# Two-block forward pass on one core: the second mixer's convolution offset, decay masks and time-step chain, rewritten and reordered

## What is computed

```python
CHUNK, SSM_HEADS, SSM_HEAD_DIM, D_STATE, CONV_WIDTH = 128, 16, 64, 128, 4
def causal_depthwise_conv(u, w, b):
    y = lax.conv_general_dilated(u, w[:, None, :], window_strides=(1,), padding=[(CONV_WIDTH - 1, 0)], ...)
    return y + b
def segsum_exp(a):
    cs = jnp.cumsum(a, axis=-1)
    diff = cs[..., :, None] - cs[..., None, :]
    return jnp.exp(jnp.where(mask, diff, -jnp.inf))          # mask: lower triangle
def ssd_chunked(xs, dt, a_neg, bm, cm):
    xg = (xs.astype(jnp.float32) * dt[..., None]).reshape(...)
    a = jnp.transpose((dt * a_neg).reshape(...), ...)
    a_cs = jnp.cumsum(a, axis=-1)
    cb = jnp.einsum('bclgn,bcsgn->bcgls', cc, bc)
    m_mat = cb[:, :, :, None] * segsum_exp(a)
    y_diag = jnp.einsum('bcgels,bcsgep->bclgep', m_mat, xg)
    ...                                                      # and the state that chunk 0 hands to chunk 1
def hybrid_mixer(...):
    xbc = jax.nn.silu(causal_depthwise_conv(xbc, conv_w, conv_b))
    dt = jax.nn.softplus(dt.astype(jnp.float32) + dt_bias.astype(jnp.float32))
    y = ssd_chunked(xs, dt, a_neg, bm, cm) + d_skip[:, None] * xs
    y = y.reshape(...) * jax.nn.silu(z)
    y = rmsnorm(y.reshape(bsz, s, SSM_GROUPS, gsize), ssm_norm.reshape(SSM_GROUPS, gsize))
    return jnp.concatenate([attn, y], axis=-1) @ w_out
```

## Time and profile before

| | us |
|---|---|
| time, median of 3 runs (lowest, highest) | 1499.72 (1497.44, 1502.09) |
| the profiled execution's own time | 1500.76 |
| its span, first to last instruction | 1499.0 |
| TensorE busy | 1470.0 (98%) |
| VectorE, ScalarE, GpSimd busy | 953.1 (64%), 785.0 (52%), 90.8 (6%) |
| mean granted TensorE clock, share of full | 0.995 |

### The profile page before, as it was taken

The page is one execution under the profiler, slowest core; times in us unless marked ns, Lnnn a source line. Parts: engine busy times, 40 slices in busy tenths (PEclk is TensorE's granted clock), DMA queues, the critical chain, the costliest instruction groups (busy, mean ns, idle before and its releaser), DMA issues.

```text
span 1499.0 us, 19461 instructions
## 1 busy us (share of the span) xinstructions
PE 1470.0 (98%) x7541; PEld 1255.5 (84%) x7541; DVE 953.1 (64%) x1356; ACT 785.0 (52%) x1232; POOL 90.8 (6%) x94
## 2 busy tenths in 40 slices
PE   8999999999999999999999989999999999999998
PEld 8888888888888888888888978888888988888886
DVE  5698765565568867555555797655555697755553
ACT  6764454444467644544445665444445574554443
POOL 0122100000002220000000010000000010000000
PEclk9999999999999999999999999999999999999999
DMA  8643356655465435566664343566654343456551
GB/s 283 214 143 125 121 162 195 201 192 184 129 210 159 141 99 179 176 207 185 192 179 119 116 140 99 169 203 207 188 184 137 107 140 118 150 188 184 188 190 57
DMA packets 178700, 245.86 MB, mean 164 GB/s; under 512 B 18976, under 2 KB 130096, under 8 KB 178608
## 3 DMA queue, kind: packets, MB, share of 16 engines
q1 hardware_dynamic: 178416, 244.54, 52.7%
q10 hardware_dynamic: 192, 0.08, 0.0%
HBM read 243.52 MB, written 1.05 MB: 163 GB/s over the span
## 4 chain that ended last, share of the span: by engine, by line
PE 80%; DVE 13%; ACT 4%; issue 2%; DVEq 0%; ACTq 0%
PE acc L546 14%; PE acc L540 14%; PE acc L543 14%; PE misc L540 10%; PE misc L543 10%; PE misc L546 10%; DVE w_lo L1321 5%; DVE arena L1696 2%; PE misc L637 1%; PE misc L734 1%; ACT arena L1019 1%; PE misc L863 1%; ACT w_hi L952 1%; PE misc L805 1%; PE misc L686 1%
## 5 line engine op out<-in xcount | busy, mean ns | idle before, releaser
L1321 DVE TENSOR_TENSOR w_lo<-w_raw,w_hi 128x1024 fp32r<-128x1024 f32 (+3 forms) x472 | 563.3, 1205 | 319.4 <-ACT w_hi L952 317.8
L952 ACT ACTIVATE w_hi<-w_raw 128x1024 fp32r<-128x1024 f32 (+3 forms) x472 | 480.8, 1029 | 287.5 <-PE misc L546 164.1
L540 PE MATMUL acc<-w_hi,h_hi 128*128 128x512 f32 (+3 forms) x832 | 210.4, 376 | 1.0 <-ACT h_hi L991 1.0
L546 PE MATMUL acc<-w_hi,h_lo 128*128 128x512 f32 (+3 forms) x832 | 201.4, 365 | 1.4 <-DVE arena L1672 1.4
L543 PE MATMUL acc<-w_lo,h_hi 128*128 128x512 f32 (+3 forms) x832 | 201.5, 365 | 0.0
L540 PE MATMUL misc<-w_hi,h_hi 128*128 128x512 f32 x640 | 175.5, 396 | 0.0
L543 PE MATMUL misc<-w_lo,h_hi 128*128 128x512 f32 x640 | 171.5, 390 | 0.0
L546 PE MATMUL misc<-w_hi,h_lo 128*128 128x512 f32 x640 | 171.5, 390 | 0.0
L546 PEld LDWEIGHTS acc<-w_hi,h_lo 128*128 128x128 f32 x832 | 148.5, 189 | 23.3 <-DVE arena L1672 1.7
L543 PEld LDWEIGHTS acc<-w_lo,h_hi 128*128 128x128 f32 x832 | 148.9, 189 | 22.0
L540 PEld LDWEIGHTS acc<-w_hi,h_hi 128*128 128x128 f32 x832 | 144.3, 191 | 23.2 <-issue 1.8
(11 more groups left out here) (200 smaller groups left out, 1298.6 us busy)
## 6 DMA issues: line engine op xcount, KB each, us to landing
w_raw<-in_w_in SPq DMA_DIRECT2D x92, 512.0 KB, 3.8
w_raw<-in_w_gate SPq DMA_DIRECT2D x176, 256.0 KB, 2.9
w_raw<-in_w_up SPq DMA_DIRECT2D x176, 256.0 KB, 3.1
w_raw<-in_w_down SPq DMA_DIRECT2D x88, 512.0 KB, 3.6
w_raw<-in_w_out SPq DMA_DIRECT2D x40, 512.0 KB, 3.6
w_raw<-in_w_in SPq DMA_DIRECT2D x32, 388.0 KB, 3.3
w_raw<-in_w_in SPq DMA_DIRECT2D x16, 336.0 KB, 4.2
w_raw<-in_w_proj_a SPq DMA_DIRECT2D x8, 512.0 KB, 4.0
```

The costliest lines, as they stand in the source:

```text
L540: pe.matmul(dst, st[0][:, k, t * P:(t + 1) * P], rhs, start=first, stop=False)
L546: return pe.matmul(dst, st[1][:, k, t * P:(t + 1) * P], rhs, start=False, stop=last)
L952: act.activation(w_hi[:, g % RING, 0:w], w_raw[:, g % RING, 0:w], ACT.Copy)\
L1321: dve.tensor_tensor(w_lo[:, g % RING, 0:w], w_raw[:, g % RING, 0:w], w_hi[:, g % RING, 0:w].bitcast(F32), ALU.subtract)\
```

## The change

The tap 3 and offset of the convolution go to ScalarE: `channels` gets two Identity instructions with scale and bias that read the PSUM bank directly, and `convolve` loses its first two. The time step `dt` no longer multiplies the states: its logarithm is taken (a second Ln on ScalarE) and added, as a bias, inside the exponentials, so that `xdt`, the four VectorE multiplications behind it and GpSimd's four are gone, and TensorE's `y` steps read `xs`. The exponentials of the diagonal blocks become four of 128 columns with a bias of their own, in place of two of 2x128 columns. One `min` of 2x2x128 columns replaces the four subtract-and-min. The skip term becomes one multiply-add for each head in `head_pair_out`, two in place of one. The small `dt` steps move ahead of `convolve(3)` on VectorE and ahead of `channels(4)` on ScalarE; `cs` moves in TensorE's order from behind `cb1` to between two slots of `z0`, `cr0` to ahead of the first slot of `z1`. A one-element Exp is placed behind the `z0` product. The start and stop flags of the slot matmuls are derived from the slot's place; they come out the same.

```diff
@@ plan_b, TensorE's order
-        xd3 attT0 attT1 xd3 xT3 xd3 xd3 z0 xT4 xT5 z0 z0 xsT0 xsT1 xsT2 xsT3 z0 z1 cb0 cb1 cs cr0 cr1
+        xd3 attT0 attT1 xd3 xT3 xd3 xd3 z0 xT4 xT5 z0 cs z0 xsT0 xsT1 xsT2 xsT3 z0 cr0 z1 cb0 cb1 cr1
@@ TensorE, y
                     pe.wait_ge(*DV_.at(layer, f"M{i}"))
+                    if i in (0, 4):
+                        pe.wait_ge(*AC.at(layer, f"xs{2 + i // 4}"))
-                        pe.matmul(b[:, u * SP:(u + 1) * SP], E[:, 0:P], xdt[:, 0, cols], start=True, stop=True)
+                        pe.matmul(b[:, u * SP:(u + 1) * SP], E[:, 0:P], xs[:, 0, cols], start=True, stop=True)
@@ ScalarE, channels(i)
+                    for k in (2 * i, 2 * i + 1):
+                        act.activation(cv[:, k, :], b[:, (k % 2) * T:(k % 2 + 1) * T], ACT.Identity,
+                                       scale=conv[:, 36 + k:37 + k], bias=conv[:, 48 + k:49 + k])\
+                            .then_inc(*AC.mark(f"xT{i}"))
@@ ScalarE, decays(hp), in place of two Exp over 2x128
+                        for part, bias in ((0, dt_v[:, hd:hd + 1]), (2, dt_v[:, 16 + hd:17 + hd])):
+                            v = E[:, u, part * P:(part + 1) * P]
+                            act.activation(v, v, ACT.Exp, bias=bias).then_inc(*AC.mark(f"ex{hp}"))
@@ ScalarE, order
-                channels(4)
-                channels(5)
                 act.wait_ge(*DV_.at(layer, "dt_u"))
                 act.activation(dt_v, dt_v, ACT.Exp).then_inc(*AC.mark())
                 act.activation(ea, prm[:, 16:32], ACT.Exp).then_inc(*AC.mark())
                 act.wait_ge(*AC.now(layer))
                 act.activation(dt_v, dt_v, ACT.Ln, bias=1.0).then_inc(*AC.mark("dt_ln"))
+                channels(4)
+                act.wait_ge(*DV_.at(layer, "dt"))
+                act.activation(dt_v, dt_m, ACT.Ln).then_inc(*AC.mark("log_dt"))
+                channels(5)
...
+                act.activation(early[:, :], halves[:, 0:1], ACT.Exp).then_inc(*AC.mark())
@@ VectorE, exponents(hp), in place of four tensor_scalar
+                    diagonal = Ex[j % 3].rearrange("p u (b t) -> p u b t", b=3)[:, :, 0:3:2, :]
+                    own = cs[:, 0:32].rearrange("p (t h a) -> p h t a", t=NT, a=1)[:, 2 * hp:2 * hp + 2, :, :]
+                    dve.tensor_tensor(diagonal, b[:, :].rearrange("p (u t q) -> p u t q", u=2, t=NT),
+                                      bc(own, [P, 2, NT, P]), ALU.min).then_inc(*DV_.mark(f"cr{hp}"))
@@ VectorE, order
+                convolve(4)
+                b = wait_bank(layer, "cs")
+                dve.tensor_copy(cs, b[:, 0:48]).then_inc(*DV_.mark("cs"))
+                dve.wait_ge(*AC.at(layer, "log_dt"))
+                dve.wait_ge(*DV_.now(layer))
+                dve.tensor_tensor(dt_v, dt_v, cs[:, 0:32], ALU.subtract).then_inc(*DV_.mark())
...
                 convolve(5)
-                    dve.tensor_tensor(xdt[:, t, 512 * half:512 * half + 512].rearrange("p (h d) -> p h d", h=8),
-                                      b[:, :].rearrange("p (h d) -> p h d", h=8), bc(r, [P, 8, SP]), ALU.mult)\
@@ VectorE, head_pair_out(hp)
+                        dve.scalar_tensor_tensor(out=ys[:, :, cols], in0=xs[:, :, cols],
+                                                 scalar=prm[:, 32 + hd:33 + hd], in1=src, op0=ALU.mult, op1=ALU.add)\
@@ GpSimd, body_b
-                    pool.tensor_tensor(v, v, bc(dsk, [P, 8, SP]), ALU.mult).then_inc(*PO.mark("xsd"))
```

More of the change, by code:

```diff
@@ L241 @@
 READ_B.update({f"wo{i}": ("dve", f"wo{i}.t1") for i in range(2)})
-ACT_READS = ("hqT", "hfT", "qkT", "PT", "GX", "xT", "cr")
+ACT_READS = ("hqT", "hfT", "qkT", "PT", "GX", "xT", "xsT", "cr")
+PAIRS = tuple(range(8))
 def reader(block, name):
@@ L583, in run_slot @@
                         at = kk * c.ncols
-                        cells.append((acc[2 * o.pair[name] + t][:, 0:c.ncols], st, tile, t, k,
+                        cells.append((acc[2 * o.pair[name] + t][:, 0:c.ncols], st, tile, t, i == 0 and kk == 0,
+                                      i == len(c.slots) - 1 and kk == nk - 1,
                                       w_hi[:, g % RING, at:at + c.ncols], w_lo[:, g % RING, at:at + c.ncols]))
@@ L601, in sweep @@
                         pe.wait_ge(*DV_.at(layer, f"nT{n}"))
-                    for dst, st, tile, t, k, hi, lo in cells:
-                        mm = low(dst, st, tile, t, hi, k == c.ktiles - 1)
+                    for dst, st, tile, t, first, last, hi, lo in cells:
+                        mm = low(dst, st, tile, t, hi, last)
                     return mm
@@ L1234, in body_b @@
                 for i in range(4):
[L1235 to L1238, removed]
+                    turned_states(i)
                 conv_silu(2)
                 copy_product(layer, "z0", lambda t: zs[:, t, 0:512], ACT.Silu, "x")
[L1242 to L1266, removed]
+                act.activation(early[:, :], halves[:, 0:1], ACT.Exp).then_inc(*AC.mark())
@@ L1267, in body_b @@
+                for hp in range(4):
+                    decays(hp)
+                copy_product(layer, "z1", lambda t: zs[:, t, 512:1024], rms="x")
+                decays(4)
+                decays(5)
+                split_until(layer, ORD[1].before["misc", "cr6"] + LOOK)
+                group_squares(0)
+                decays(6)
+                decays(7)
                 operand(layer, "ssT0")
                 operand(layer, "ssT1")
-                split_until(layer, ORD[1].before["misc", f"y{SH // 2 - 1}"] + LOOK)
+                split_until(layer, ORD[1].before["misc", "y7"] + LOOK)
@@ L1729, in body_b @@
                 dve.tensor_tensor(dt_v, dt_u, dt_a, ALU.min).then_inc(*DV_.mark("dt_u"))
-                convolve(4)
+                convolve(3)
                 dve.wait_ge(*AC.at(layer, "dt_ln"))
-                dve.tensor_tensor(dt_m, dt_m, dt_v, ALU.add).then_inc(*DV_.mark("dt"))
+                dve.scalar_tensor_tensor(out=dt_m, in0=dt_u, scalar=1e-37, in1=dt_v, op0=ALU.max, op1=ALU.add)\
+                    .then_inc(*DV_.mark("dt"))
                 dve.wait_ge(*DV_.now(layer))
```

116 lines of the change are left out of this document (62 added, 54 removed).

## The result

The changed kernel takes 1489.47 us (median of 4 runs, 1488.46 to 1489.76); runs of the kernel before, made beside it, take 1498.58 (1497.31 to 1502.09). The ratio is 0.9934, with a 95% interval of 0.9921 to 0.9947. The prediction said 1489.7 and a range of 1485.5 to 1495.5.

What follows compares the result with a forecast made beforehand. TensorE, busy 98% of the span, was taken as the bound, so only its gaps and half-clock stretches could yield: 4.4 + 6.1 = 10.5 us off 1500.76, less half of 1.04, gives 1489.7 us, range 1485.5 to 1495.5.

Steps and rivals of the forecast that it cites:

- The stretch: TensorE from `xsT0` to `y1`, second mixer: 20.25 us in layer 1 instead of 26.33; gains 4.4 and 6.1, together 10.5.
- The first Silu: ScalarE ahead of `xsT0`: Silu starts 8.7 us after the last `xd3` copies, as now, at 877.3 to 877.7.
- The wait ahead of xsT3: New TensorE wait of 1.45 us per layer for VectorE's copy of `cs`, ends 0 and 2.0; rival without it, chance 0.06.
- cb0, cr1, y0: TensorE's waits ahead of `cb0` and `cr1` go; `y0` has slack 1.3 us; rival, `y0` waits 1.7 per layer, chance 0.10.
- The clock: Rival: TensorE's clock still falls to half behind the `xsT3` wait, 1.6 us a layer, 1491.3 or 1492.9; chance 0.18.
- The attention part: Identities of `channels(0)` to `(2)` near `O4`: cost 0, range -0.3 to 1.6 us; rival 1492.9 to 1495, chance 0.07.
- The step on `xsT0`: TensorE ahead of `xsT0`: Identities use up the early `dt`'s gain; `cs` (0.59 us) fills the idle 0.76 there.
- the one on GpSimd: GpSimd's multiplications go at no price, nothing waits for them; VectorE beside them gets 1.7 us back.
- The 1.7: VectorE time regained: two lo took 4.05 us beside GpSimd's multiplications, 2.35 elsewhere.
- The sum: Total over both layers: 10.5 us off the profiled 1500.76 gives 1490.3, then half of 1.04 off: 1489.7 us.
- The table loads: ScalarE: next activation 1.30 us after a load starts, no 1.38 draining; rival, extra loads make it slower, chance 0.04.

Runs made afterwards that it cites:

- the kernel without waits: Changed kernel with tap 3 and offset back on VectorE and the copy of `cs` no longer behind one slot's lo: 1484.85 us.
- the first experiment: Changed kernel with one slot's lo no longer ahead of VectorE's copy of `cs`: 1485.76 us.
- The experiments on the one minimum and the early Exp: Changed kernel with four 128-column minimum steps in place of one of 512: 1489.9 us; changed kernel without the one-element Exp: 1490.14 us.

## Why the prediction was right, and where it was not

**The stretch: right.** 20.25 us were forecast, 20.18 and 20.19 measured; 10.5 us of gain forecast, 10.65 measured. Two small errors cancel in it: the work itself is 18.10 us by the kernel without waits, not 18.95 - 0.59 = 18.36, and the 0.2 that TensorE takes to run again was left out for the wait ahead of `xsT3`. The time, 1489.7 against 1489.47, agrees more closely than the runs can tell, and that is luck: the forecast was 10.0 below a median of 1499.72, the measured gain is 9.1 from a median of 1498.58, and taking off half of the 1.04 between the profiled execution and the median was a choice.

**The first Silu: right.** 8.7 us behind the last `xd3` copies were forecast; it is 876.72 - 867.91 = 8.81 in ScalarE's timeline:

```profile
867.91 1.06 ACT L1070 ACTIVATE arena<-acc,small 128x388 f32<-128x388 f32 x2 [0.86 <-PE acc L547]
...
872.88 1.01 ACT L1200 ACTIVATE arena<-misc,conv 128x256 f32<-128x256 f32 x2
...
875.43 1.28 ACT L1206 ACT_TABLE_LOAD   x1
876.72 2.00 ACT L1206 ACTIVATE arena<-arena 128x1024 f32<-128x1024 f32 x2
```

An Identity takes 565 ns on average and steps by about 0.45, where 0.40 was taken and 0.37 to 0.48 were the ends. The Trainium skill (ScalarE: Activation LUTs, What ACT_TABLE_LOAD costs) prices each operand that is a pointer at about 93 ns; with two of them and 256 columns an estimate by its figures is 585 ns, which this trace bears out.

**The wait ahead of xsT3: right.** 1.45 forecast, 1.33 and 1.32 measured, and by the first experiment the copy of `cs` is its cause. The price of its place is more than the wait: 3.7 us in the medians, 3.0 of them in the two stretches; the rest is no more than the runs' spread.

**cb0, cr1, y0: right.** M ends at 892.0 and TensorE is at `y0` at 893.04, a slack of 1.0 where 1.3 was said. The forecast had no lo ahead of M, which holds only by the edit to the exponents of pair 1 shown above. The chain on ScalarE held: the decays began at 888.80 (889.3 forecast), and the four new Exp step by 0.29 where 0.25 was taken. The experiments on the one minimum and the early Exp use up 0.4 and 0.2 of the slack without harm.

**The clock: the rival did not come.** A wait of 1.33 left the granted clock at 1.00; so did 1.37 ahead of `cr0` with 0.99 ahead of `y0`, and 1.6 ahead of `y0` alone. It fell behind waits of 4.87 and 3.71. In between, equal waits came out differently in the two layers of one run. Two of 1.5 in the kernel before were followed by 0.50 in layer 0; in layer 1 they left the clock at 1.00, and it fell behind a third, of 1.66, that ended at 1247.22:

```profile
1240.00:1247.00 7.00, 4.10 (x22) 3.08 (x21) 5.36 (x18) 3.34 (x9) 0.00 (x0) 1.00 0.45 150
1248.00:1249.00 1.00, 1.00 (x7) 1.00 (x6) 0.72 (x1) 0.24 (x1) 0.00 (x0) 0.50 0.00 0
```

With GpSimd's work cut and the order moved, 1.88 ahead of `cr0` left it at 1.00 in layer 0, and 1.87 was followed by 0.50 in layer 1. With `cr0` left behind `cb1`, 2.24 ahead of `cb0` left it at 1.00 in layer 0, and 2.26 was followed by 0.50 in layer 1. So the length of a wait does not say by itself whether the clock falls. That it would hold was the likelier case, not a thing the rows of before could show.

**The attention part: right, though its row looks worse.** `O4` is listed with a wait of 0.71 in place of 0.18:

```profile
853.51 1.10 PE L664 MATMUL misc<-arena 128*128 128x64 f32 x8 [0.71 <-ACT arena L1029]
```

But `O0` to `O5` takes 857.02 - 832.29 = 24.73 us in place of 24.59. The wait has taken over from one of 0.15 ahead of `O3`, which is gone, and the price is 0.14 in this layer against a forecast of 0; layer 1's attention part lies in the stretch of 324.40 before and 324.32 after. A longer wait in the list is no loss until the steps around it start later.

**Where the reasoning failed: the share of the parts.** The step on `xsT0` ended with "Taking `cs` out of the later stretch is the gain", and the one on GpSimd with "at no price", beside 1.7 us that VectorE gets back. The runs show the reverse. With the products cut most of the gain (6.4 of 9.1 us) is there in the old order, and with them whole the same moves lose 3.1 us. The 1.7 came from the two lo in the earlier trace rows alone; the taps of `convolve(5)` ran beside the same multiplications in the kernel before (3.53 us for the six, 2.71 in the earlier trace rows), so it was 2.5 already there, and it becomes 3.0 where the moved order puts all of `convolve(5)` beside GpSimd. The sum held because it went by when each step of the changed kernel could start, and there the products are gone; by the same reasoning the moves alone were expected at 1490 to 1491, and they took 1502.74.

**The table loads: right.** The next activation starts 876.72 - 875.43 = 1.29 us after a load starts, as before the change, and no extra loads came in with Identity. No run here shows the 1.38 of draining of which the prediction speaks.

## What to carry to other kernels

Price an instruction on GpSimd by what it does to VectorE's instructions beside it, and look at those one by one: in the moved order products with idle time on their own engine cost 6 us of a 1500 us kernel. Before moving a step forward, ask what its reader is queued behind. The copy of `cs` stood behind a helper's weight step that it did not need, and a bank wait carried that to TensorE for 1.5 us in each layer. Where a wait is for two engines, do not trust the name in the list; look which of the two also moves when the wait does.

## What the runs showed of the hardware

Beside GpSimd's multiplications (128x512, both inputs in SBUF), two VectorE `tensor_scalar` of 256 columns took 2.26 us in place of 0.73, and six multiply-adds 4.16 in place of 2.71; with GpSimd's work cut, both were back. The Trainium skill (SBUF — State Buffer, SBUF: two separate sides) says that VectorE, in a 2-port mode or with two inputs in SBUF, and GpSimd share a port pair as an exclusive lock, one blocking the other for a whole instruction. These rows agree that the neighbours slow VectorE; they don't show which instruction waited for which, nor which of the two conditions the `tensor_scalar`, with one input in SBUF, met.

A minimum over 2x2x128 columns from PSUM, with a broadcast second operand, took 0.68 us; the same as four `tensor_scalar` of 128 columns took 1.12.
